# Sixteen heads' query and key rows: the on-chip transfers issued by GpSimd instead of SyncE, keys of both heads ahead of the queries

## What is computed

```
k = rms_norm((h @ w_k) per head);  q = rms_norm((h @ w_q) per head)
F = cumsum(log_sigmoid(h @ w_f + b_f))
logits = (q . k) / sqrt(64) + F[t] - F[s]     # causal
p = softmax(logits);  out = p @ v
```

## Time and profile before

| | |
|---|---|
| three runs | 1284.01, 1284.07, 1279.84 us; median 1284.01 |
| the profiled execution | 1285.45 us, its span 1283.7 us |
| busy share of PE, PEld, DVE, ACT, POOL | 94%, 78%, 61%, 37%, 2% |
| mean granted clock of TensorE | 0.975 |
| where the on-chip transfers of pairs 0 to 7 are issued | from 641.3 to 860.4 us of the span |
| issued on SP in all | 112 on-chip transfers, 248 weight and modulation loads, 11 small ones, 8 stores |

### The profile page before, as it was taken

The page is one execution under the profiler, slowest core; times in us unless marked ns, Lnnn a source line. Parts: engine busy times, 40 slices in busy tenths (PEclk is TensorE's granted clock), DMA queues, the critical chain, the costliest instruction groups (busy, mean ns, idle before and its releaser), DMA issues.

```text
span 1283.7 us, 16841 instructions
## 1 busy us (share of the span) xinstructions
PE 1211.0 (94%) x5802; PEld 1001.5 (78%) x5802; DVE 777.5 (61%) x1100; ACT 480.9 (37%) x781; POOL 25.4 (2%) x37
## 2 busy tenths in 40 slices
PE   4399999999999999999888999998999999999998
PEld 2288888888888888889667877877888888888887
DVE  5755698785665665557866777774764343443441
ACT  4222232542231331424545666653442232241331
POOL 2000000000000000001200000000000000000000
PEclk9699999999999999999988999999999999999999
DMA  9355565365655655333133444432233333333333
GB/s 341 120 184 190 185 194 180 117 210 181 200 195 172 215 171 161 90 91 85 50 99 88 113 109 122 117 97 66 66 95 91 94 97 99 98 98 98 99 88 92
DMA packets 227807, 168.73 MB, mean 131 GB/s; under 512 B 5828, under 2 KB 206700, under 8 KB 227756
## 3 DMA queue, kind: packets, MB, share of 16 engines
q1 hardware_dynamic: 227196, 165.88, 43.4%
q10 hardware_dynamic: 528, 2.10, 0.5%
q0 software_dynamic: 32, 0.07, 0.0%
HBM read 153.24 MB, written 2.10 MB: 121 GB/s over the span
## 4 chain that ended last, share of the span: by engine, by line
PE 78%; DVE 11%; ACT 4%; DMA 3%; issue 3%; SPq 2%; DVEq 0%; ACTq 0%
PE bank L528 24%; PE bank L530 23%; PE bank L529 23%; PE bank L793 2%; DVE ada_acc L1391 1%; DVE w_lo L1264 1%; SPq L397 1%; PE bank L740 1%; PE bank L775 1%; DMA q<-qk_hi 1%; ACT w_hi L924 1%; DMA raw<-in_sc_w_in 1%; DVE h_lo L1308 1%; DVE ta L1299 1%; DVE tc L1299 1%
## 5 line engine op out<-in xcount | busy, mean ns | idle before, releaser
L528 PE MATMUL bank<-h_hi,w_hi 128*128 128x512 f32 (+1 forms) x872 | 342.6, 393 | 24.1 <-DVE h_lo L1308 21.7
L529 PE MATMUL bank<-h_lo,w_hi 128*128 128x512 f32 (+1 forms) x872 | 332.8, 382 | 0.0
L530 PE MATMUL bank<-h_hi,w_lo 128*128 128x512 f32 (+1 forms) x872 | 332.7, 381 | 0.0
L924 ACT ACTIVATE w_hi<-raw 128x1024 fp32r<-128x1024 f32 x192 | 202.0, 1052 | 264.1 <-DMA raw<-in_mlp_w 218.0
L1264 DVE TENSOR_TENSOR w_lo<-raw,w_hi 128x1024 fp32r<-128x1024 f32 x192 | 234.7, 1223 | 56.0 <-ACT w_hi L924 50.9
L528 PE MATMUL bank<-g_hi,w_hi 128*128 128x512 f32 (+1 forms) x688 | 262.2, 381 | 3.0 <-DVE g_lo L1308 2.1
L530 PE MATMUL bank<-g_hi,w_lo 128*128 128x512 f32 (+1 forms) x688 | 258.4, 376 | 0.0
L529 PE MATMUL bank<-g_lo,w_hi 128*128 128x512 f32 (+1 forms) x688 | 258.2, 375 | 0.0
L528 PEld LDWEIGHTS bank<-h_hi,w_hi 128*128 128x128 f32 x872 | 165.1, 189 | 63.9 <-issue 25.0
L529 PEld LDWEIGHTS bank<-h_lo,w_hi 128*128 128x128 f32 x872 | 165.3, 190 | 33.6 <-issue 3.6
L530 PEld LDWEIGHTS bank<-h_hi,w_lo 128*128 128x128 f32 x872 | 165.0, 189 | 31.6
(11 more groups left out here) (164 smaller groups left out, 1019.8 us busy)
## 6 DMA issues: line engine op xcount, KB each, us to landing
raw<-in_mlp_w SPq DMA_DIRECT2D x128, 512.0 KB, 4.0
ada_raw<-in_ada_w SPq DMA_DIRECT2D x40, 1024.0 KB, 5.9
raw<-in_sc_w_in SPq DMA_DIRECT2D x24, 512.0 KB, 3.9
ada_first<-in_ada_w SPq DMA_DIRECT2D x16, 512.0 KB, 8.8
raw<-in_w_kv SPq DMA_DIRECT2D x16, 512.0 KB, 4.1
raw<-in_sc_w_out SPq DMA_DIRECT2D x8, 512.0 KB, 3.9
raw<-in_q_w SPq DMA_DIRECT2D x8, 512.0 KB, 4.0
k<-qk_hi SPq DMA_DIRECT2D x32, 128.0 KB
```

The lines of the kernel that those rows point to most:

```text
L528: mm(out[:, cols], weights_hi, hi[:, k, cols], start=(k == 0), stop=False)
L529: mm(out[:, cols], weights_hi, lo[:, k, cols], start=False, stop=False)
L530: return mm(out[:, cols], weights_lo, hi[:, k, cols], start=False, stop=(k == KT - 1))
L924: go(w_hi[:, jj, :, :], raw[:, jj, :, :], ACT.Copy).then_inc(hi_ok, 1)
```

## The change

All 112 on-chip transfers go from SP's program to POOL's, behind the six small operations by which POOL makes `f_parts`. Their order changes too: both heads' keys first, then both heads' queries. The waits (`k_ok`, `q_ok`, `s_ok`) go along. SP keeps the weight loads alone.

```diff
             for (kind, j), b in BLOCK_OF.items():
-                freed = KVQ_ORDER[b - KVQ - 4] if b - KVQ >= 4 else None
-                if freed == ("q", 0):
-                    head_keys(0, 0)
-                    head_keys(0, 1)
-                if freed == ("q", 1):
-                    head_queries(0, 0)
-                    head_queries(0, 1)
-                if freed and freed[0] == "k" and freed[1] >= 2:
-                    pair(freed[1] - 1)
                 sp.wait_ge(pe_done, b - 3)
...
             for n in range(KT):
-                if n == 1:
-                    pair(KT - 2)
-                if n == GROUP:
-                    pair(KT - 1)
                 sp.wait_ge(pe_done, OUT + n - 3)
...
+            def copy(to, of):
+                return pool.dma_start(to.bitcast(F32), of.bitcast(F32))
+
+            def head_keys(j, half):
+
+                own, other = OWN[half], OWN[1 - half]
+                pool.wait_ge(k_ok, j + 1)
+                if j:
+                    pool.wait_ge(s_ok, TT * (2 * j - 1 + half))
+                copy(k1[own, half, :], qk_hi[own, 1, :]).then_inc(head_in[half], 16)
+                copy(k1[other, half, :], qk_hi[own, 1, :]).then_inc(head_in[half], 16)
+                copy(k2[own, half, :], qk_lo[own, 1, :]).then_inc(head_in[half], 16)
+                if j == 0:
+                    pool.wait_ge(fg_ok, 1)
+                    pool.wait_ge(pads_ok, 4)
+                h = 2 * j + half
+                copy(k2[other.start:other.start + 3, half, :], f_parts[h:h + 65:32, :]).then_inc(head_in[half], 16)
+
+            def head_queries(j, half):
+
+                own, other = OWN[half], OWN[1 - half]
+                pool.wait_ge(q_ok, j + 1)
+                if j:
+                    pool.wait_ge(s_ok, TT * (2 * j - 1 + half))
+                copy(q1[own, half, :], qk_hi[own, 0, :]).then_inc(head_in[half], 16)
+                copy(q1[other, half, :], qk_lo[own, 0, :]).then_inc(head_in[half], 16)
+                copy(q2[own, half, :], qk_hi[own, 0, :]).then_inc(head_in[half], 16)
+
+            for j in range(KT):
+                for half in range(2):
+                    head_keys(j, half)
+                for half in range(2):
+                    head_queries(j, half)
```

More of the change, by code:

```diff
@@ L395, in _ @@
             mlp(0, MLP0)
[L396 to L427, removed]
-            for (kind, j), b in BLOCK_OF.items():
-                freed = KVQ_ORDER[b - KVQ - 4] if b - KVQ >= 4 else None
-                if freed == ("q", 0):
-                    head_keys(0, 0)
-                    head_keys(0, 1)
-                if freed == ("q", 1):
-                    head_queries(0, 0)
-                    head_queries(0, 1)
-                if freed and freed[0] == "k" and freed[1] >= 2:
-                    pair(freed[1] - 1)
+            for (kind, j), b in BLOCK_OF.items():
                 sp.wait_ge(pe_done, b - 3)
```

## The result

The changed kernel takes 1303.34 us (median of four runs, 1301.76 to 1304.28), against 1284.04 us for the kernel before: 1.0156 times as long, interval 1.0132 to 1.018. It is 19 us slower. The profiled execution took 1304.28 us, its span is 1302.0 us, 18.3 more than before.

What follows compares the result with a forecast made beforehand. PE was taken to bound the attention, without slack for late transfers. Stalls 48.8, pair 0 2.8 and slower clock 18.0 sum to 69.6 us on 1285.45, giving 1355 us; range 1308 to 1382 (main forecast's own 1335 to 1372).

Steps and rivals of the forecast that it cites:

- PE would wait at the even heads' logits, each microsecond in full: Line 765, pairs 1 to 7: PE has no slack, so later query transfers stall it fully; 48.8 us more idle.
- POOL's step: Time per transfer issue on POOL: taken as `wf_raw`'s 1.03 us, bounded below by SP's 0.635; ten issues make 10.3 us.
- the forecast's own sum: Pairs 1 to 7: ten issues plus landing give data 13.4 us after `k_ok`; 7 x 13.4 - 45.0 = 48.8 us.
- The landing: Even head's last query transfer, from POOL's issue to landing: taken as 3.1 us, between 2.8 and 4.3.
- The clock, 18 us: Behind 7 us stalls PE's granted clock drops to half; six new drops at 3.0 us make 18 us.
- Pair 0, 2.8 us: Pair 0's last query transfer lands at 658.3 instead of 655.50, delaying the chain through ACT to PE by 2.8 us.
- Collisions: Earlier q-block weight loads beside the pair's transfers: costed at nothing, up to 1 us a pair; as rival 1362 us, chance 0.05.
- The cheap-issue rival: POOL's step is only SP's 0.635 us: stalls of 2.5 us, 1304 to 1322, about 1310 us; chance 0.15.
- At most some 4 us could be gained: Attention: upper limit on gain, from PE's four transfer waits (2.0 us) and ACT's wait passing to PE at pair 1.

Runs made afterwards that it cites:

- e4: Changed kernel with 16 small fills on POOL between keys and queries of pairs 1 to 7, lengthening PE's stalls; 1343.97 us, ratio 1.047.
- e6: Changed kernel with the forget gate's weights (`wf_raw`) fetched in four transfers instead of one; one run, 1301.5 us.
- e3: Changed kernel with SP holding the weight load that before stood behind a pair's transfers until those have landed; 1299.14 us, ratio 1.0122.
- e2: Changed kernel with POOL issuing in the order of before (head by head from pair 1 on), loads still free; 1291.1 us, ratio 1.0056.
- e7: Changed kernel with both the order of before and SP's loads held until the pair's transfers have landed; 1285.6 us, ratio 1.001.
- e1: Kernel before, transfers still on SP, but both heads' keys issued ahead of both heads' queries; 1307.66 us, ratio 1.0182.

## Why the prediction was wrong

- **PE would wait at the even heads' logits, each microsecond in full: right.** Seven waits, 14.7 us more, and e4's added 4.1 us a pair came through whole.
- **POOL's step: the step that failed.** "I bound the step from below by SP's 0.635 us and take 1.03, since it is the same engine and queue": the step is 0.52 us. Ten of them are 5.15 us, not 10.3. The only row of POOL was another shape, and e6 shows that its price came from its many pieces. The lower bound was wrong too: SP's price said nothing about POOL's. With 0.52 and the measured 0.28 + 2.9 the forecast's own sum gives data at 8.4 us: 7 x 8.4 - 45.0 = 13.8 us instead of 48.8.
- **The landing** (3.1 taken) was nearly right: 2.9 to 3.0 us in pairs 2 to 7. The start of POOL 0.28 us behind its semaphore, 2 us in all, was not in the sum.
- **The clock, 18 us: none came**, since the stalls are 2 us instead of 7. Only pair 7 pays 1.3 us more, and 1.2 come back later. This failed with the step before it, not by itself.
- **Pair 0, 2.8 us: the right size for a wrong reason.** The issues are quicker than SP's (last one 2.6 us behind the first, against 3.1), but the landing took 5.37 us beside weight loads.
- **Collisions were costed at nothing**, with the q block's request "about 6 us after `k_ok`". So it falls in pair 3 (751.62, 6.15 us behind the low part of k), but in pair 1 it comes half a microsecond behind it, and pair 0's load was not looked at. They cost 4.2 us (e3), or 5.5 in e2's order (1291.1 - 1285.6), mostly in pairs 0 and 1, where a load is no longer behind the transfers.
- **The cheap-issue rival** named the case (stalls of 2.5 us, 1304 to 1322, 1310 likeliest) and got 0.15. It took SP's price as the step, so even its lower end lies just above the result, and the stated range began at 1308.
- **"At most some 4 us could be gained"**: nothing in the runs contradicts it.

The parts, each as a difference of medians: the order 13.5 us (e3 - e7), the freed loads 4.2 (changed kernel - e3), the engine 1.1 (e7 - before): 18.8 of 19.3, and the rest is what the medians of before differ by. The parts depend on each other: with the loads free the order costs 12.2 (changed kernel - e2). On SP the same order costs 23.5, since its steps are longer and the clock falls behind some of the stalls.

## What to carry to other kernels

Where an engine arrives just when the data does, count how many issues stand ahead of the last transfer it waits for: the place in the queue cost 13.5 us here, the engine that issues 1.1. A single row of an engine's transfer prices only its own shape; when the shape differs, the nearest row of another engine is no bound, and the range must go below both. And a queue that holds a load back behind small transfers may be protecting them: when one is freed, ask what its loads will run beside.

## What the runs showed of the hardware

- A 64 x 2 KB on-chip copy is issued by POOL in 0.52 us and by SP in about 0.6 (0.635 with the gap); a copy of three rows takes 0.51 to 0.52 on POOL and 0.70 to 0.72 on SP in pairs 1 to 7.
- POOL starts 0.28 us after the DVE operation that it waits for ends, SP 0.02.
- Such a copy, as the last query transfer, lands mostly 2.6 to 3.1 us after POOL's issue, 2.34 to 2.37 after SP's, and 4 to 6 us after POOL's beside weight loads that were issued before it.
- Waits of PE of 2.0 us left the granted clock at full (2.4 GHz) in pairs 2 to 6. In e1 two waits of 2.5 us behind the same work at full clock ended differently, one at full and one at half (1.2 GHz). Waits of 6.2 to 6.9 us dropped it to half in all seven pairs, at 2.4 to 2.6 us for each of the five that were not slow before.
